# The odd layer's output projection moved into the spatial stage's block: weights loaded into buffers already free, m loaded in three pieces, the last group's transposes between the first row blocks

## What is computed

```python
def odd_project(x, g_norm, w_in, g_v):
    h = rms_norm(x, g_norm)
    p = jnp.einsum('bld,dc->blc', h, w_in)
    u, v, gate = jnp.split(p, 3, axis=-1)
    return jax.nn.gelu(u), layer_norm(jax.nn.gelu(v), g_v), gate

def chunk_spatial(v, w_s, b_s):
    L = v.shape[1]
    w = jnp.where(jnp.tril(jnp.ones((L, L), dtype=bool))[None], w_s[:, :L, :L], 0.0).astype(v.dtype)
    return jnp.einsum('gts,nsgc->ntgc', w, v) + b_s[:, :L].T.astype(v.dtype)[None, :, :, None]

def odd_output(x, u, sv, gate, w_out):
    return x + jnp.einsum('blc,cd->bld', u * sv * jax.nn.silu(gate), w_out)
```

## Time and profile before

| | |
|---|---|
| Median of three runs | 2446.04 us (2444.86 to 2446.36) |
| Profiled execution: span from the first to the last instruction | 2443.4 us; the runs' median is 2.6 us above it |
| PE busy | 2247.8 us (92%) |
| DVE, ACT, POOL busy | 967.1, 924.4, 643.8 us |
| Mean granted PE clock | 0.955 of full speed |

### The profile page before, as it was taken

How to read it: one execution, slowest core, us unless ns; L and a number is a source line. 1 busy time by engine, 2 the same in 40 slices (tenths; PEclk the granted TensorE clock), 3 DMA queues, 4 the chain that set the end, 5 groups by cost and what they waited for, 6 DMA issues and landing times. The chain is left out here.

```text
span 2443.4 us, 30994 instructions
## 1 busy us (share of the span) xinstructions
PE 2247.8 (92%) x11248; PEld 1816.3 (74%) x11248; DVE 967.1 (40%) x1501; ACT 924.4 (38%) x1456; POOL 643.8 (26%) x386
## 2 busy tenths in 40 slices
PE   6999999899999788999999699699999999995999
PEld 5999999777777566666666378477778888773687
DVE  3334444453853856777776610310023211111000
ACT  4233332223443334777776510422233333334100
POOL 1222112220220000456555641111231111123420
PEclk8999999999999889999999899699999999997999
...
DMA packets 257337, 287.93 MB, mean 118 GB/s; under 512 B 69498, under 2 KB 168700, under 8 KB 257084
## 3 DMA queue, kind: packets, MB, share of 16 engines
...
...
## 5 line engine op out<-in xcount | busy, mean ns | idle before, releaser
L226 PE MATMUL bank<-whi,x_hi 128*128 128x512 f32 (+1 forms) x1536 | 592.5, 386 | 21.3 <-POOL wlo L206 16.1
L228 PE MATMUL bank<-wlo,x_hi 128*128 128x512 f32 (+1 forms) x1536 | 579.4, 377 | 0.0
L230 PE MATMUL bank<-whi,x_lo 128*128 128x512 f32 (+1 forms) x1536 | 579.0, 377 | 0.0
L226 PEld LDWEIGHTS bank<-whi,x_hi 128*128 128x128 f32 x1536 | 292.9, 191 | 83.7 <-POOL wlo L206 20.6
L259 ACT ACTIVATE projected<-bank 128x512 f32<-128x512 f32 (+1 forms) x160 | 92.2, 576 | 620.2 <-PE bank L230 590.9
L230 PEld LDWEIGHTS bank<-whi,x_lo 128*128 128x128 f32 x1536 | 292.5, 190 | 42.0
L228 PEld LDWEIGHTS bank<-wlo,x_hi 128*128 128x128 f32 x1536 | 293.4, 191 | 39.3 <-issue 0.7
L2358 POOL TENSOR_TENSOR dec_v_lo<-dec_v,dec_v_hi 128x1024 fp32r<-128x1024 f32 x92 | 230.1, 2523 | 220.7 <-ACT dec_v_hi L2712 220.6
L206 POOL TENSOR_TENSOR wlo<-wraw,whi 128x512 fp32r<-128x512 f32 (+1 forms) x192 | 230.5, 1233 | 32.0 <-ACT whi L199 31.9
L2527 DVE TENSOR_TENSOR dec_kt_lo<-bank,dec_kt_hi 128x512 fp32r<-128x512 f32 x256 | 170.6, 684 | 100.5 <-ACT dec_kt_hi L2702 100.0
L2702 ACT ACTIVATE dec_kt_hi<-bank 128x512 fp32r<-128x512 f32 x256 | 150.5, 596 | 106.9 <-PE bank L2386 95.7
...
## 6 DMA issues: line engine op xcount, KB each, us to landing
dec_k<-cache_k SPq DMA_DIRECT2D x256, 256.0 KB, 3.9
dec_v<-cache_v SPq DMA_DIRECT2D x256, 256.0 KB, 4.2
wraw<-w_in_even SPq DMA_DIRECT2D x32, 512.0 KB, 6.7
wraw<-w_in_odd SPq DMA_DIRECT2D x16, 1024.0 KB, 8.9
...
m<-gm_mt ACTq DMA_DIRECT2D x8, 1056.0 KB, 4.1
...
```

Source lines behind the costliest of these rows:

```text
L226: pe.matmul(bank[:, 0:width], e.xhi[:, k, c:c + P], e.whi[:, k, 0:width], start=(k == 0), stop=False)
L228: pe.matmul(bank[:, 0:width], e.xhi[:, k, c:c + P], e.wlo[:, k, 0:width], start=False, stop=False)
L230: mm = pe.matmul(bank[:, 0:width], e.xlo[:, k, c:c + P], e.whi[:, k, 0:width], start=False, stop=(k == KD - 1))
```

## The change

`out_block` is gone. Its work stands in `second_out_stage`, which gives each engine a few functions, and `spatial_block` calls these at the end of the engines' own code, in the same block.

Its buffers overlay those of the spatial stage. The high and low weight parts k = 0 to 7 take the place of the projection's x, the four raw weight slots that of the projection's raw weights, the m tiles of the first two row blocks (`mhi`, `mlo`) that of the projection's split weights; k = 8 to 15 and the rest take that of the stage's other tiles. Each first write is placed behind the last use of what lay there: the raw slots behind POOL's last split, `whi0` and the m tiles behind the last projection, the rest behind `gated(7)` and `turn(7)`.

m is loaded for both first row tiles in three pieces: k = 0 to 11 (groups 0 to 5) behind the last projection, k = 12 and 13 (group 6) and k = 14 and 15 (group 7) when these groups are stored. It lands in `mlo`; ACT copies the high part to `mhi`, DVE subtracts in place.

PE, after `mix_v(7)`, goes through the weight rows for the first two row tiles alone; the small sample mix of group 7 comes after k = 1 and `turn(7)` after k = 4. The sample's 64 matmuls come after k = 15. For the other six tiles there is one m buffer for each of two slots, and DVE makes all low parts.

```diff
-def out_block(nc, e, name, kt, w_dram, m_dram, residual, target):
...
+OUT_SLOTS = 4
+MIX_SAMPLE_AFTER, TURN_LAST_AFTER, TURN_LAST_BEFORE = 1, 4, 8
...
+def second_out_stage(nc, e, ctx, kt, w_dram, m_dram, residual, target, ends):
...
+    weight_tiles(range(early))
+    ms_raw = sb("ms_raw", [P, kt, NS])
+    wraw = [sb(f"wraw{i}", [P, D]) for i in range(OUT_SLOTS)]
+    mhi, mlo = [None, None], [None, None]
+    for i in range(2):
+        mhi[i] = sb(f"mhi{i}", [P, kt, P], F32R)
+        mlo[i] = sb(f"mlo{i}", [P, kt, P], F32R)
+    weight_tiles(range(early, kt))
+    ms = sb("ms", [P, kt, 2 * NS], F32R)
+    x = [sb(f"x{i}", [P, D]) for i in range(2)]
+    y_sample = sb("y_sample", [NS, D])
+    y = [sb(f"y{i}", [P, D]) for i in range(2)]
+    pieces = [(0, kt - 4), (kt - 4, kt - 2), (kt - 2, kt)]
...
+    ob = [Banks(c, 6 * i, e.banks[6 * i:6 * i + 2], 2, rounds=pairs) for i in range(2)]
+    sample_bank = Banks(c, 2, e.banks[2:4], 2, rounds=1)
...
+    def sync(sp, store_last_v):
+        def weights(k):
+            if k >= OUT_SLOTS:
+                sp.wait_ge(w_lo.sem, w_lo.at(k - OUT_SLOTS, 1))
+            sp.dma_start(wraw[k % OUT_SLOTS][:], w_dram[P * k:P * k + P, :]).then_inc(w_landed[k % OUT_SLOTS].sem, 16)
+        def first_tiles(i):
+            k0, k1 = pieces[i]
+            for slot in range(2):
+                c0 = NS + P * slot
+                sp.dma_start(mlo[slot][:, k0:k1, :].bitcast(F32), m_view[:, k0:k1, c0:c0 + P]).then_inc(
+                    piece_landed[i].sem, 16)
+        def residual_rows(tile, slot, use):
+            sp.wait_ge(ob[slot].free[1].sem, ob[slot].free[1].at(use, 0))
+            sp.dma_start(x[slot][:], residual(tile, False)).then_inc(x_landed[slot].sem, 16)
+        def body(tile, slot, use):
+            sp.wait_ge(ob[slot].full[1].sem, ob[slot].full[1].at(use, 0))
+            sp.dma_start(mlo[slot][:].bitcast(F32), m_view[:, :, ds(tile * P + (NS - P), P)]).then_inc(m_landed[slot].sem, 16)
+            residual_rows(tile, slot, use)
+        sp.wait_ge(ends.w_ready.sem, ends.w_ready.at(NG, 0))
+        for k in range(OUT_SLOTS):
+            weights(k)
+        ends.wait_projected(sp)
+        ends.wait_groups(sp, NG - 2)
+        first_tiles(0)
+        store_last_v()
+        ends.wait_groups(sp, NG - 1)
+        first_tiles(1)
+        for k in range(OUT_SLOTS, kt - 4):
+            weights(k)
+        ends.wait_groups(sp, NG)
+        first_tiles(2)
+        sp.dma_start(ms_raw[:], m_view[:, :, 0:NS], allow_slow_non_contiguous=True).then_inc(ms_landed.sem, 16)
+        for k in range(kt - 4, kt):
+            weights(k)
+        ends.wait_gated(sp)
+        for slot in range(2):
+            residual_rows(slot + 1, slot, 0)
+        sp.dma_start(y_sample[:], residual(0, True)).then_inc(xs_landed.sem, 16)
+        with sp.Fori(1, pairs) as pair:
+            body(pair * 2 + 1, 0, pair)
+            body(pair * 2 + 2, 1, pair)
...
+    def act_weights(act, k):
+        act.wait_ge(w_landed[k % OUT_SLOTS].sem, w_landed[k % OUT_SLOTS].at(k // OUT_SLOTS, 16))
+        act.activation(whi[k][:], wraw[k % OUT_SLOTS][:], ACT.Copy).then_inc(w_hi.sem, 1)
+    def act_pieces(act, i):
+        k0, k1 = pieces[i]
+        act.wait_ge(piece_landed[i].sem, piece_landed[i].at(0, 32))
+        for slot in range(2):
+            act.activation(mhi[slot][:, k0:k1, :], mlo[slot][:, k0:k1, :].bitcast(F32), ACT.Copy).then_inc(
+                piece_hi.sem, 1)
+    def scalar_first(act):
+        act_weights(act, 0)
+    def scalar_fill(act):
+        act_weights(act, 1)
+        act_pieces(act, 0)
+    def scalar_rest(act, turn_last):
...
+        for k in range(2, kt):
+            if k == 5:
+                act_pieces(act, 1)
+            if k == TURN_LAST_BEFORE:
+                turn_last()
+            if k == kt // 2 + 2:
+                ends.wait_gated(act)
+            if k == kt - 4:
+                act.wait_ge(ends.tail.written(4), ends.tail.written_by(0, 4))
+                act.wait_ge(ends.v_stored.sem, ends.v_stored.at(NG, 0))
+            if k == kt - 2:
+                ends.wait_groups(act, NG)
+            act_weights(act, k)
+            if k == kt - 3:
+                act_pieces(act, 2)
+        act.wait_ge(ms_landed.sem, ms_landed.at(0, 16))
+        act.activation(ms[:, :, 0:NS], ms_raw[:], ACT.Copy).then_inc(ms_ready.sem, 1)
+        for slot in range(2):
+            store(slot + 1, slot, 0)
+        for slot in range(2):
+            split(1, slot)
+        for half in range(2):
+            act.wait_ge(sample_bank.read(half), sample_bank.read_by(0, half))
+        act.dma_start(target(0, True), y_sample[:]).then_inc(ys_stored.sem, 16)
...
+    def tensor_open(pe):
+        for half in range(2):
+            for slot in range(2):
+                pe.wait_ge(ob[slot].read(half), ob[slot].read_before(0, half))
+    def tensor_k(pe, k):
+        for i, (k0, _) in enumerate(pieces):
+            if k == k0:
+                pe.wait_ge(piece_lo.sem, piece_lo.at(i, 2))
+        pe.wait_ge(w_lo.sem, w_lo.at(k, 1))
+        for slot in range(2):
+            for half in range(2):
+                three(pe, slot, half, k, k == kt - 1)
+    def tensor_tail(pe):
...
+        pe.wait_ge(ms_ready.sem, ms_ready.at(0, 2))
+        for half in range(2):
+            bank, cols = sample_bank.bank(half), slice(BANK * half, BANK * half + BANK)
+            pe.wait_ge(sample_bank.read(half), sample_bank.read_before(0, half))
+            for k in range(kt):
+                pe.matmul(bank[0:2 * NS, :], ms[:, k, :], whi[k][:, cols], start=(k == 0), stop=False)
+                mm = pe.matmul(bank[0:2 * NS, :], ms[:, k, :], wlo[k][:, cols], start=False, stop=(k == kt - 1))
+            mm.then_inc(sample_bank.written(half), 1)
+        with pe.Fori(1, pairs) as pair:
+            body(pair * 2 + 1, 0, pair)
+            body(pair * 2 + 2, 1, pair)
+    def vector_lows(dve, i):
+        k0, k1 = pieces[i]
+        for slot in range(2):
+            dve.wait_ge(piece_hi.sem, piece_hi.at(i, slot + 1))
+            dve.tensor_tensor(mlo[slot][:, k0:k1, :], mlo[slot][:, k0:k1, :].bitcast(F32),
+                              mhi[slot][:, k0:k1, :].bitcast(F32), ALU.subtract).then_inc(piece_lo.sem, 1)
+    def vector_more(dve):
+        for i in range(1, len(pieces)):
+            vector_lows(dve, i)
...
-        mb = Banks(c, 2, e.banks[2:8], 10)
+        mb = Banks(c, 2, e.banks[2:8], 10, rounds=NG - 1)
         c.close(NG)
+        tail = Banks(c, 2, e.banks[2:6], 10, rounds=1)
+        c.close(1)
+        ctx.close()
+        e.layer.close()
+        ends = SpatialEnds(e.w_ready, e.w_last, m_ready, v_stored, out_stored, tail)
+        out_sync, (out_first, out_fill, out_rest), out_gpsimd, (out_open, out_k, out_tail), (
+            out_lows, out_more, out_vector) = second_out_stage(
+            nc, e, outer, KG, a["w_out_odd"][0], a["m1"], residual, target, ends)
...
-                store_v(NG - 1)
+                out_sync(sp, lambda: store_v(NG - 1))
...
-                mix_v(0)
-                with pe.Fori(1, NG) as r:
+                mix_v(0, mb, 0)
+                mix_sample(mb, 0)
+                with pe.Fori(1, NG - 1) as r:
                     pe_project(pe, e, r, UG)
-                    turn(r - 1)
-                    mix_v(r)
-                turn(NG - 1)
+                    turn(r - 1, mb, r - 1)
+                    mix_v(r, mb, r)
+                    mix_sample(mb, r)
+                pe_project(pe, e, NG - 1, UG)
+                turn(NG - 2, mb, NG - 2)
+                mix_v(NG - 1, tail, 0)
+                out_open(pe)
+                for k in range(KG):
+                    out_k(pe, k)
+                    if k == MIX_SAMPLE_AFTER:
+                        mix_sample(tail, 0)
+                    if k == TURN_LAST_AFTER:
+                        turn(NG - 1, tail, 0)
+                out_tail(pe)
...
-                with dve.Fori(1, NG) as r:
-                    gated(r - 1)
+                with dve.Fori(1, NG - 1) as r:
+                    gated(r - 1, mb, r - 1)
                     norm_v(r)
-                gated(NG - 1)
+                gated(NG - 2, mb, NG - 2)
+                norm_v(NG - 1)
+                out_lows(dve)
+                gated(NG - 1, tail, 0)
+                out_more(dve)
+                out_vector(dve)
...
                 act_store(act, e, NG - 1, UG, split=False)
-                turn(NG - 2)
+                out_first(act)
+                turn(NG - 2, mb, NG - 2)
+                out_fill(act)
                 prepare(NG - 1)
-                turn(NG - 1)
-                act.wait_ge(out_stored.sem, out_stored.at(NG, 0))
+                out_rest(act, lambda: turn(NG - 1, tail, 0))```

SP's DMA queue, before, from the last instruction of the group loop (`gm_v` is v, `out1_x1` and `out1_y` hold the sample's m and the first tile's m):

```order
L2865 DMA gm_v<-gv 128x9x256
L2876 REGISTER_ALU
L2876 COMPARE_AND_BRANCH
```

(24 more changed lines are left out.)

301 lines of the change are left out of this document (113 added, 188 removed).

## The result

The changed kernel takes 2415.91 us (median of four runs, 2411.99 to 2419.92); the kernel before took 2446.2 us in the same measurement. The ratio is 0.9875, 95% interval 0.9859 to 0.9891: 30 us faster, against 31.6 us forecast. The profiled execution of the changed kernel took 2414.78 us with a span of 2413.0.

A forecast was written before the change was run, and what follows sets the result against it. PE, busy 92%, bounds the kernel; only its waits and half clock can give time, 43 us at most. Steps from 2199.3 sum to 2407.9 against 2439.5, 31.6 less: 2446.04 becomes 2414.4 us, range 2408 to 2425.

The forecast's parts named there:

- likeliest case: Whole kernel: PE's old waits mostly filled with row-block work; 2414.4 us, own range 2410 to 2418, chance 0.64.
- the sum: All steps added from the last projection's end at 2199.3: 2407.8 or 2407.9 against 2439.5, 31.6 us less.
- First piece: Ahead of k = 0: first m load landed 8.2 us after the last projection, then 4.8 us of splitting.
- Half clock, 2.5: At k = 0 and 1, after PE's wait: 5 us at half clock, 2.5 us lost (bounds 0 and 3).
- More comes back: Rival: piece lands in 5.8 us, clock recovers before it matters, `wlo3` isn't slowed; 2408 with all three; chance 0.12.
- Wait on POOL, 1.6 at k = 3: Ahead of k = 3: PE waits 1.6 us for `wlo3`, POOL's low weight part, ready at 2225.3.
- Slowed by DVE: At `wlo3`: DVE's 2.29 us operation on two SBUF tiles overlaps POOL's subtraction, which loses 1.9 us.
- DVE's bank reads: During `gated(7)`: their slowing of POOL was bounded by nothing and 2.2 us; nothing was taken.
- k = 12, no wait: At k = 12: `wlo12` ready at about 2249.5, PE comes at 2251.9, so no wait; slack 2.4 us.
- less comes back: Rival: late piece, bank reads slowing POOL, slow group 7 store; one some 2417, all 2422.7, new gap 2426; chance 0.19.
- Tail: After k = 15: sample matmuls to 2277.3 cover row tile 3, ready 2271.5, at worst 2276.1; third wait goes.
- Slower: Rival: short waits at each k keep half clock through the first row blocks; 2450 us, chance 0.03.

The follow-up runs named there:

- the run with 13 filling matmuls: Changed kernel plus 13 matmuls that nothing reads, filling PE's wait ahead of k = 0; 2414.3 us, ratio to before 0.9868.
- The run with the tail alone: Kernel before, with only later tiles' m in its own slot, DVE's low parts and sample matmuls behind k = 15; 2439.3 us, ratio 0.9977.

## Why the prediction was right, point by point

The time lies inside the likeliest case's own range (2410 to 2418), and the stage is 0.4 us from the sum. Part of that closeness is luck: PE starts k = 5 32.7 us after the projection (2233.54), 0.9 ahead of the sum's 33.6, and what follows gives back half. The profiled span is 1.2 us above the 2411.8 forecast, since the projection ended 1.7 us later than in the trace of before. By its own steps:

**First piece.** 8.2 for the landing was 7.6 (ACT starts at 2208.49), 4.8 for the split was 5.2. k = 0 starts 12.8 us after the projection, against 13.0. From issue to landing the piece took 7.13 us by the chain's row. The fit of the Trainium skill that the prediction quoted (DMA: Bandwidth & Descriptors, "Anatomy of one DMA — SWDGE (gpsimd) path"; 5.6 us, for another DMA path) was too short by 1.5.

**Half clock, 2.5.** This term was mis-used. k = 0, k = 1 and the sample mix lost 2.0 us to it, but the prediction had `wlo2` ready at 2220.9, just when PE would come, so by its own steps a faster clock could bring nothing. "More comes back" counted 2.5 us for it all the same; the run with 13 filling matmuls got the clock at k = 0 and 1 and no time. That rival reached no lower than about 2410.

**Wait on POOL, 1.6 at k = 3.** It was 1.0 at k = 4, with 0.15 at k = 2. The cause was the one named, DVE's 2.29 us operation on two SBUF tiles, and the size nearly so: a low part lost 2.03 us, 1.9 forecast. But it hit the next one, because here the operation that started second stood still: DVE first waited out POOL's k = 3, then POOL's k = 4 waited out DVE. "Slowed by DVE" was half of it. That DVE's bank reads don't slow POOL was chosen rightly: beside them k = 2 took 2.40 us, and they took 3.23, as before.

**k = 12, no wait.** Right, with 0.3 us of slack and not 2.4. The store of group 7 was issued at 2234.45, and SP went on at 2242.2: 7.8 us, not 4.1. Weight loads were under way beside it; that they caused it is not shown. This part of "less comes back" happened, and the slack paid for it, with a store issued 1.1 us earlier after the projection than the sum had it.

**Tail.** Right: the sample's matmuls cover row tile 3, whose load took 9.0 us (issued 2262.58, ACT at 2271.62), near the worst case of 10.4. The run with the tail alone gave its 9.3 us.

**Slower.** The clock stayed at 1.00 in every stretch from 2220 to 2400, in spite of the wait of 1.0 us at k = 4.
